# A routed expert block on one core: first biases turned on VectorE, a bias product inside the loop, last rows by a one-hot product, and a gather without empty places

## The reference, cut to what matters

```
logits = h @ router_w + router_b          # 512 x 32
top_val, top_idx = top_k(logits, 4)       # four experts for each token
gate = softmax(top_val)
for each expert e, on its tokens:
    u = h[tokens] @ w1[e] + b1[e]         # 1024 -> 2048, first bias
    g, lin = min(u[:, :1024], 7), clip(u[:, 1024:], -7, 7)
    y = ((lin + 1) * g * sigmoid(1.702 * g)) @ w2[e] + b2[e]
    out[tokens] += gate * y
x = x + g2 * out                          # g2 comes from the condition vector
```

## Time and profile before

| | us |
|---|---|
| median of 3 runs | 2125.63 (2125.32 to 2132.86) |
| profiled execution, its own time | 2124.19 |
| its span | 2122.5 |
| TensorE busy | 1951.7 (92%) |
| VectorE / ScalarE / GpSimd busy | 639.0 / 365.9 / 195.5 |
| granted clock, mean over the span | 0.965 |

### The profile page before, as it was taken

How to read it: one execution, slowest core, us unless ns; L and a number is a source line. 1 busy time by engine, 2 the same in 40 slices (tenths; PEclk the granted TensorE clock), 3 DMA queues, 4 the chain that set the end, 5 groups by cost and what they waited for, 6 DMA issues and landing times.

```text
span 2122.5 us, 37796 instructions
## 1 busy us (share of the span) xinstructions
PE 1951.7 (92%) x15926; PEld 1045.7 (49%) x15926; DVE 639.0 (30%) x1668; ACT 365.9 (17%) x823; POOL 195.5 (9%) x240
## 2 busy tenths in 40 slices
PE   5999999998999999999998888889898888989989
PEld 4576655753444444444343433434343343765854
DVE  6346757322120202122121111202020115257240
ACT  2115631432110101011000000101000011142110
POOL 1020000000002121211111111110101010000000
PEclk8979999999899999999999999999999989999999
DMA  9711222321579999999999999999999984200001
GB/s 301 225 47 60 80 80 80 159 75 64 204 258 385 384 390 374 385 380 361 383 370 377 377 372 376 371 374 369 376 369 370 339 263 130 80 1 1 1 0 40
DMA packets 155314, 510.96 MB, mean 241 GB/s; under 512 B 22098, under 2 KB 99272, under 8 KB 105992
## 3 DMA queue, kind: packets, MB, share of 16 engines
q1 hardware_dynamic: 132112, 472.94, 60.2%
q0 software_dynamic: 17088, 26.48, 5.8%
q10 hardware_dynamic: 5944, 9.09, 1.2%
HBM read 489.47 MB, written 18.48 MB: 239 GB/s over the span
## 4 chain that ended last, share of the span: by engine, by line
PE 63%; SPq 15%; DMA 14%; DVE 4%; issue 2%; ACT 1%; POOL 0%; ACTq 0%; DVEq 0%; POOLq 0%
PE bank L1417 14%; DMA ring<-in_exp_w_dram 13%; PE bank L390 10%; PE bank L1433 8%; PE bank L398 7%; SPq L888 7%; PE bank L793 5%; SPq L892 4%; PE bank L552 3%; SPq L883 3%; PE bank L574 2%; PE bank L563 2%; PE bank L764 1%; PE bank L374 1%; DVE arena L740 1%
## 5 line engine op out<-in xcount | busy, mean ns | idle before, releaser
L1417 PE MATMUL bank<-ring,arena 128*32 128x512 f32 x5696 | 643.0, 600 | 72.3 <-DMA ring<-in_exp_w_dram 69.0
L1417 PEld LDWEIGHTS bank<-ring,arena 128*32 128x32 f32 x5696 | 180.0, 111 | 511.7 <-issue 359.2
L1433 PE MATMUL bank<-ring,arena 128*32 128x256 f32 x5696 | 325.3, 386 | 24.5 <-DMA ring<-in_exp_w_dram 15.9
L1789 DVE COPY arena<-bank 128x12 f32<-128x12 f32 (+2 forms) x32 | 5.4, 170 | 911.9 <-PE bank L1381 880.1
L1433 PEld LDWEIGHTS bank<-ring,arena 128*32 128x32 f32 x5696 | 217.3, 111 | 122.8 <-DMA ring<-in_exp_w_dram 22.1
L390 PE MATMUL bank<-hT,ring 128*128 128x512 f32 x448 | 210.3, 622 | 13.2 <-DVE hT L770 7.5
L1036 POOL DMA_INDIRECT expert_sums<-arena,dst_r x89 | 137.9, 1550 | 380.3 <-ACT arena L1172 355.2
L398 PE MATMUL bank<-ring,hT 128*128 128x256 f32 (+1 forms) x768 | 156.4, 363 | 0.0
L390 PEld LDWEIGHTS bank<-hT,ring 128*128 128x128 f32 x448 | 87.7, 199 | 119.3 <-issue 115.8
L1154 ACT ACTIVATE arena<-bank 128x384 f32<-128x384 f32 (+2 forms) x64 | 26.5, 464 | 693.2 <-PE bank L1398 693.2
L398 PEld LDWEIGHTS bank<-ring,hT 128*128 128x128 f32 x768 | 135.6, 190 | 18.4 <-issue 2.4
(11 more groups left out here) (325 smaller groups left out, 1551.9 us busy)
## 6 DMA issues: line engine op xcount, KB each, us to landing
ring<-in_exp_w_dram SPq DMA_DIRECT2D x384, 1024.0 KB, 26.0
ring<-in_ada_w_dram SPq DMA_DIRECT2D x24, 1024.0 KB, 10.9
ring<-in_w_in_dram SPq DMA_DIRECT2D x23, 1024.0 KB, 9.9
ring<-in_w_out_dram SPq DMA_DIRECT2D x8, 1024.0 KB, 4.9
arena<-in_exp_b_dram SPq DMA_DIRECT2D x128, 64.0 KB
expert_sums<-arena POOLq DMA_DIRECT2D x5, 512.0 KB, 4.7
arena<-in_x_dram ACTq DMA_DIRECT2D x1, 2048.0 KB, 12.5
ring<-in_w_in_dram SPq DMA_DIRECT2D x8, 256.0 KB, 5.0
```

The source lines that it names most:

```text
L1417: mm = pe.matmul(bank[g][QUAD * c:QUAD * (c + 1), :].rearrange("p (h n) -> p h n", h=2), rowsT[:, k, QUAD * g:QUAD * (g + 1)], w[:, :, SW ...
L1433: mm = pe.matmul(bank[4 + g // 2][QUAD * c:QUAD * (c + 1), SW * (g % 2):SW * (g % 2 + 1)], actT[:, j, g, QUAD * q:QUAD * (q + 1)], w[:, c, :],
```

## The change

- First biases: the 128 bias transfers and SP's wait ahead of them go. Four transfers before the loop bring all of `exp_b1` as rows of experts; VectorE turns them once in blocks of 32x32 (`b1T`), and in each iteration reads the expert's number from `order_i` into a register, copies 16 columns and turns them, broadcast, into `b1_rows` (`biases`), ahead of `targets`.
- Second biases: the eight products of L1523 move into iterations 10 to 17, one in each, into bank 7, between the first layer and `spread`; VectorE adds each to the residual at the head of its iteration, and `turn_rows`, which also writes bank 7, waits for that. The eight products by the identity of L1527 become transposes.
- The last expert's rows are not scattered. ScalarE scales them into `y_last`, VectorE builds a one-hot matrix of tokens (`hot_last`), TensorE multiplies both in four row quarters into eight banks, VectorE adds these to the residual. ScalarE reads the sums back after the last but one expert's scatter; TensorE branches after VectorE's additions.
- Gather: the table holds token number minus 512 and VectorE adds 512, so an empty place gives 512, beyond the bound of 511, and the gather leaves it out. `xg` is zeroed once.

```diff
-            def bias_in(e, n, signal):
-                for c in range(4):
-                    sp.dma_start(b1_all[n][QUAD * c:QUAD * (c + 1), :].rearrange("p (e h n) -> p e h n", e=1, h=2),
-                                 b1_cols[c, bass.ds(e, 1), :, :].unsqueeze(0).to_broadcast([QUAD, 1, 2, SW]))\
-                      .then_inc(signal, 16)
...
-            bias_in(0, 0, b1_in[0])
+            for c in range(4):
+                sp.dma_start(b1_rows[QUAD * c:QUAD * (c + 1), :].rearrange("p (h n) -> p h n", h=2), b1_cols[c])\
+                  .then_inc(b1_in, 16)
...
-                if n >= 2:
-                    sp.wait_ge(main.u_in, n - 1)
-                bias_in(e, n % 2, b1_in[n % 2])
...
-                pool.indirect_dma_start(xg[0:rows, :], None, h2_dram, bass.IndirectOffsetOnAxis(src_i[0:rows, 0:1], 0))\
+                pool.indirect_dma_start(xg[0:rows, :], None, h2_dram, bass.IndirectOffsetOnAxis(src_i[0:rows, 0:1], 0),
+                                        bounds_check=S - 1, oob_is_err=False)\
                     .then_inc(sg.got, 16)
...
+            link(pool.memset(xg, 0.0))
...
-                if n >= 1:
+                if 1 <= n < NEXP:
                     put(main, n, PARTS_BY[n - 1], dst_r[(n - 1) % 4], QUADS[n - 1])
...
-            act.wait_ge(main.free, NEXP)
+            act.wait_ge(main.dst, NEXP)
+            act.wait_ge(main.y, NEXP)
+            for g in range(QUADS[-1]):
+                act.activation(y_last[:, g, :], bank[4 + g // 2][:, SW * (g % 2):SW * (g % 2 + 1)], ACT.Copy,
+                               scale=meta_r[(NEXP - 1) % 4][:, g, 2:3]).then_inc(y_last_ok, 1)
+            act.wait_ge(main.free, NEXP - 1)
...
+                if n in B2_AT:
+                    t = n - B2_AT[0]
+                    pe.wait_ge(main.at_ok, 2 * n)
+                    pe.matmul(bank[7][:, :], b2_keep[:, P * t:P * (t + 1)], gatesT, start=True, stop=True)\
+                      .then_inc(b2_t, 1)
...
+                    if n in B2_AT:
+                        pe.wait_ge(b2_ok, n - B2_AT[0] + 1)
                     turn_rows(main, 16 * (n + 2), QUADS[n + 1])
...
-            pe.wait_ge(main.y_ok, PARTS_BY[NEXP])
+            pe.wait_ge(main.u_in, NEXP)
+            pe.wait_ge(main.at_ok, 2 * NEXP)
+            pe.wait_ge(hot_last_ok, 1)
+            pe.wait_ge(y_last_ok, QUADS[-1])
+            for j in range(2):
+                for g in range(QUADS[-1]):
+                    for c in range(4):
+                        rows = slice(QUAD * c, QUAD * (c + 1))
+                        mm = pe.matmul(bank[2 * c + j][:, :], y_last[rows, g, P * j:P * (j + 1)], hot_last[rows, g, :],
+                                       start=(g == 0), stop=(g == QUADS[-1] - 1))
+                mm.then_inc(last_t, 1)
+            pe.wait_ge(last_ok, ND)
...
-            pe.wait_ge(gT_ok, 1)
-            for t in range(ND):
-                pe.matmul(bank[t][:, :], b2_keep[:, P * t:P * (t + 1)], gatesT, start=True, stop=False)
...
-                    mm = pe.matmul(bank[t][:, i * P:(i + 1) * P], y_rows[i][:, P * t:P * (t + 1)], ident[:, :],
-                                   start=False, stop=(i == NT - 1))
+                    mm = pe.transpose(bank[t][:, i * P:(i + 1) * P], y_rows[i][:, P * t:P * (t + 1)], ident[:, :])
...
-            dve.tensor_copy(route[:, :, :, 0], tb)
+            dve.tensor_scalar(route[:, :, :, 0], tb, -float(S), None, ALU.add)
...
-                dve.tensor_copy(src_i[0:rows, :], meta[0:rows, 0:1]).then_inc(sg.src, 1)
+                dve.tensor_scalar(src_i[0:rows, :], meta[0:rows, 0:1], float(S), None, ALU.add).then_inc(sg.src, 1)
...
+            def biases(sg, e):
+                settle(sg, dve.tensor_copy(b1_one.unsqueeze(2), b1T[:, :, bass.ds(e, 1)]))
+                settle(sg, dve.transpose(b1_rows.rearrange("p (k q) -> p k q", q=QUAD),
+                                         bc(b1_one.unsqueeze(2), [P, 16, QUAD])))
...
+            dve.wait_ge(b1_in, 64)
+            link(dve.transpose(b1T.rearrange("p k e -> p (k e)"), b1_rows))
             for n in range(NEXP):
+                if n in B2_AT:
+                    t = n - B2_AT[0]
+                    dve.wait_ge(b2_t, t + 1)
+                    dve.scalar_tensor_tensor(out=resT[:, t, :], in0=bank[7][:, :], scalar=mod[:, 40 + t:41 + t],
+                                             in1=resT[:, t, :], op0=ALU.mult, op1=ALU.add).then_inc(b2_ok, 1)
+                if n == 0:
+                    e = 0
+                else:
+                    e = dve.value_load(order_i[0:1, n:n + 1], min_val=0, max_val=NEXP - 1)
+                biases(main, e)
...
+            to_last = meta_r[(NEXP - 1) % 4]
+            for g in range(QUADS[-1]):
+                for i in range(NT):
+                    ins = dve.tensor_scalar(hot_last[:, g, P * i:P * (i + 1)], iota_c[:, :], float(P * i), to_last[:, g, 1:2],
+                                            ALU.add, ALU.is_equal)
+            ins.then_inc(hot_last_ok, 1)
+            dve.wait_ge(b2_ok, ND)
+            for j in range(2):
+                dve.wait_ge(last_t, j + 1)
+                for t in range(j, ND, 2):
+                    dve.scalar_tensor_tensor(out=resT[:, t, :], in0=bank[t][:, :], scalar=mod[:, 40 + t:41 + t],
+                                             in1=resT[:, t, :], op0=ALU.mult, op1=ALU.add).then_inc(last_ok, 1)
```

More of the change, by code:

```diff
@@ L166, in two_block_layer @@
         route = room(4608, [NT, NEXP, 4])
-        b1_all = [room(5120 + 512 * n, [512]) for n in range(2)]
+        b1T, b1_rows, b1_one = room(5120, [16, NEXP]), room(5632, [512]), room(7808, [16])
         u_in = room(OM + 1024, [4, 512])
+        y_last, hot_last = u_in[:, 0, :].rearrange("p (g n) -> p g n", g=2), u_in[:, 2:4, :]
         posmT = room(OM + 1024, [S], NEXP)
@@ L273, in two_block_layer @@
         w1_used, w2_used = sem("w1_used"), sem("w2_used")
-        b1_in = [sem("b1_in0"), sem("b1_in1")]
+        b1_in = sem("b1_in")
         places_in, repl_ok, pos_ok, perm_ok, turned_ok, order_ok = (
@@ L281, in two_block_layer @@
         y_used = sem("y_used")
+        b2_t, b2_ok = sem("b2_t"), sem("b2_ok")
+        hot_last_ok, y_last_ok, last_t, last_ok = (sem(n) for n in ("hot_last_ok", "y_last_ok", "last_t", "last_ok"))
         f_t, f_ok, f_out = sem("f_t"), sem("f_ok"), sem("f_out")
@@ L825, in dve_out @@
                 ins.then_inc(res_ok, 1)
+        B2_AT = range(10, 10 + ND)
+        assert QUADS[-1] == 2
         OUT_PARTS = ((0, 4), (4, 6), (6, 8))
@@ L1793, in targets, with swiglu @@
                 dve.tensor_tensor(dst[:, 0:quads], dst_f[:, 0:quads], slot_base[:, 0:quads], ALU.add).then_inc(sg.dst, 1)
-            def swiglu(sg, n, bias, quads):
+            def biases(sg, e):
+                settle(sg, dve.tensor_copy(b1_one.unsqueeze(2), b1T[:, :, bass.ds(e, 1)]))
+                settle(sg, dve.transpose(b1_rows.rearrange("p (k q) -> p k q", q=QUAD),
+                                         bc(b1_one.unsqueeze(2), [P, 16, QUAD])))
+            def swiglu(sg, n, quads):
                 for g in range(quads):
-                    ins = dve.tensor_tensor(u_in[:, g, :], bank[g][:, :], bias, ALU.add)
+                    ins = dve.tensor_tensor(u_in[:, g, :], bank[g][:, :], b1_rows, ALU.add)
                 ins.then_inc(sg.u_in, 1)
@@ L1890, in _ @@
                     at = dve.value_load(pos_i[0:1, 0:1], min_val=0, max_val=NEXP - 1)
+                    of = dve.value_load(exp_i[0:1, 0:1], min_val=0, max_val=NEXP - 1)
+                    biases(over, of)
                     dve.tensor_copy(route_o[:, :, :], route[:, :, bass.ds(at, 1), :].rearrange("p i e c -> p i (e c)"))
@@ L1898, in _ @@
                     targets(over, o + 1, meta_r[0], dst_r[0], 4)
-                    dve.wait_ge(over_in, o * (16 * (SLOTS + 4)) + 16 * (SLOTS + 4))
+                    dve.wait_ge(over_in, o * (16 * SLOTS) + 16 * SLOTS)
                     dve.wait_ge(over.u, o + 1)
-                    swiglu(over, o + 1, b1_all[0], 4)
+                    swiglu(over, o + 1, 4)
             dve.wait_ge(y_used, NT)
```

16 lines of the change are left out of this document (8 added, 8 removed).

## The result

The changed kernel takes 2053.62 us, the median of four runs (2049.77 to 2055.15), against 2125.48 for the kernel before on the same chip (2125.16 to 2132.86). The ratio is 0.9651, with a 95% interval of 0.9626 to 0.9676: 3.5% faster, a gain of 72 us where the sum above has 32.4. The profiled execution took 2054.17 us, its span is 2052.4.

The account below looks back on a forecast made before the run. TensorE was taken to bind up to about 960 us, the DMA engines after. 24.5 + 5 - 4 - 2 + 8.9 = 32.4 us off 2124.19 gave 2091.8, forecast as 2093 us, range 2072 to 2114.

Parts of the forecast that it names:

- What bounds the kernel: Expert loop: TensorE binds to about 960 us, DMA engines after; at most 85 us can be won by relieving DMA.
- Part 1: Expert loop: 7680 bias packets of 1 KB leave the DMA engines, at 51 ns each 24.5 us won.
- rival A: Whole kernel: relief passes whole, with even engines, nothing lost early and fast transposes; 45 us won, 2079; chance 0.15.
- Part 2: Gather in the expert loop: 800 empty rows of 4 KB skipped, 0 to 10 us won, 5 taken.
- rival D: Gather: leaving places out puts the rest on fewer engines and weights wait; slower, 2156; chance 0.05 with an unseen cause 0.06.
- Part 3: Loop up to about 960 us: TensorE binds, so part of the saved DMA time is lost; 4 us written off.
- Part 4: Iterations 10 to 17: bias product delays the second layer 2.2 us each, 18 over eight, mostly covered; 2 us charged.
- a cover of 19: Iterations 10 to 17: TensorE's idle time, 27 us, shrinking to 19 after the DMA relief, hides the bias product's stall.
- Part 5: Tail after the last expert product: one-hot product and transposes take 20.5 us against 29.4; 8.9 us won.
- 36 as the sign for the forecast: Expert loop after 1001 us: twelve weight slots in about 36 us instead of 37.2 would show the forecast right.
- B's picture: Iterations 10 to 17: TensorE takes over, waits for VectorE replace ring waits; 2111, at the upper end 2121; chance 0.12.
- C: Expert loop: small packets cost nothing, slipping in between weights, so only the tail is won; 2117; chance 0.07.

Follow-up runs that it names:

- every_fourth: The kernel before with its four bias transfers an expert each written to every fourth of 128 partitions instead of 32 neighbours; 2084.04 us, ratio 0.9794.
- tail_and_b2_only: The kernel before with only the second biases' product in iterations 10 to 17 and the new tail, biases and gather as before; 2117.8 us, ratio 0.9943.
- after_b2_late: The changed kernel with the second biases' product in iterations 22 to 29 and VectorE's biases step ahead of its wait for it; 2050.9 us, ratio 0.9627.
- own_rows_32: The kernel before with each partition of the four bias transfers reading another expert's bias, still into 32 neighbouring partitions; 2126.95 us, ratio 1.0001.
- bias_only: The kernel before with only the first biases held in SBUF and turned on VectorE; 2066.73 us, ratio 0.9705.
- after_hoist: The changed kernel with only VectorE's biases step moved ahead of its wait for the second biases' product; 2050.76 us, ratio 0.9640.
- gather_all_128: after_hoist with every gather issued over all 128 partitions, added places left out by the bounds check; 2036.31 us, ratio 0.9568.

## Why the prediction fell short

**What bounds the kernel: right.** The loop was bound by the DMA engines from 960 us on, the 85 us of ring waits were the ceiling, and 67 of them went. But the sentence that four issues fewer save "only what their packets cost the engines" is where the error enters: it has no room for a cost that a packet puts on others. (Its 120 issues are right for the loop; 124 went in all, four of them ahead of it.)

**Part 1, the bias transfers: the step that failed.** The term was 24.5 us, from 51 ns a packet taken in a stretch in which nothing but 1 KB packets flew. Measured: 62.7 in all, of which the packets' own part is 20 (by bytes I had 21), and 43 are weights slowed beside them. Neither the forecast nor rival A had this in it, since both multiply a packet's own time. I took the price of the packets from a stretch without weights, and read the share of 1.03 as useful work; but it is the same at 373 and at 393 GB/s, so it also counts what a packet loses to others. The trace of before could have told. These are the 15 us slices of GB/s from 1001 to 1601 us, first of before, then of every_fourth:

```profile
GB/s 352 420 336 390 372 370 398 350 400 349 379 383 359 386 341 398 397 355 390 343 386 385 360 393 345 386 373 369 382 359 398 362 368 381 357 375 359 379 389 353
```
```profile
GB/s 388 419 389 386 390 387 393 397 421 383 393 389 385 392 397 421 379 399 386 388 389 399 421 386 386 382 388 382 399 418 372 398 386 385 381 397 415 378 402 386
```

Before dips to 336 to 353 every few slices; every_fourth, with the same bias packets, never goes under 372. Finer stretches of before tell what the dips are. I cut 1001 to 1601 us into pieces of 3 us and leave out those with traffic of queue 0 (gathers and scatters, a share of 1% or more). The 48 pieces without packets of 1 KB (fewer than five) carry 418 GB/s in the mean, the 53 with them 367. From 1136 to 1139 us, for one, it is 426, and from 1139 to 1142, where 102 of these packets fly, 338. In every_fourth the same means are 417 and 420 (40 and 59 pieces). 53 pieces are 9.9 us for each of 16 experts; at a rate 12% lower that is 1.2 us an expert, 38 over 31 of them, an estimate that leaves out the pieces with gathers and comes near the 43.

On VectorE's side the estimates held: the transpose took 0.71 us (0.65 taken), and the register load left no gap that the trace shows, L1883 ending at 1004.23 and the copy L1822 starting at 1004.22, where I had put 1.0.

**Part 2, the gather: right in size,** 4.7 us (interval 2.3 to 7.2) for the 5 taken. The 800 rows are gone as bytes, but each leaves a packet under 512 B, which the sum did not have. That leaving places out might load few engines (rival D) did not come true. That the gather's destinations cost another 15 us was not in it, and the change doesn't touch that.

**Part 3, TensorE early: right in kind.** 700 to 960 us is at 257.7 of 260 us, no better than before. The 4 us written off for it were not measured by themselves.

**Part 4, the bias product: the cover was wrong, the 2 us are not refuted.** I charged 2 us against a cover of 19. With the relief of 63 instead of 24.5 the cover was gone: TensorE is busy 255.8 us of 260 in 960 to 1220. In tail_and_b2_only, with the weights still the bound, the stall shows no loss (12.1 us won, 9.9 of them in the tail). The stall was shorter than computed, 1.4 us over the usual gap instead of 2.2, but the iterations had a second price that I did not write down: a granted clock of 0.50 for some 3 us, and second layers 1.7 us longer, in all eight (three of eleven are so without the product, in after_b2_late). That is at most 3.1 us an iteration, 25 in all, against a cover that was no longer there. The medians have no more than 5 of them as lost gain (79.5 against 74.2), and taking the product out of these iterations (after_b2_late) gave no more than 5 either. That the slots that filled meanwhile were used later is the likely reason.

**Part 5, the tail: right.** 9.6 us won for 8.9, with the one-hot passes at 0.116 us, VectorE's sums at 5.36 and the transposes 1.2 us faster than taken (5.83 us at a mean clock of 0.63, at 0.50 for the first half). The next layer's weights did not come late.

**Rivals and signs.** Twelve slots take 600 / 217 x 12 = 33.2 us; I had named 36 as the sign for the forecast, and 37.2 for no effect. TensorE's ring waits are 18 us, not 50. By my own list that is beyond the forecast towards B's picture, waits for VectorE in their place (10.7 us), but at a gain no case had. A, at 2079 the nearest, is 25 us above the measured time; C, packets at no cost, has the costly term at nothing. The range was too narrow because its good end, A, was built from the same term as the forecast: I priced the term from a stretch of small packets alone and by its bytes at the mean rate, and neither holds what the weights lose beside it.

## What to carry to other kernels

Where transfers share saturated engines, price a small transfer by what the big ones lose, not by its own packets: two sets of short stretches of one trace, with and without it, and the GB/s at an unchanged share show it (418 and 367 here). Give side transfers destinations that spread over all 128 partitions, even by every fourth partition or with a list of places that are left out. And when a change relieves one bound by more than a few per cent, recompute every edit that was hidden under it. All of this is one kernel's evidence.

## What the runs showed of the hardware

- A transfer into 32 neighbouring partitions slows the weight stream beside it: 256 KB an expert cost 20 us over the kernel by their bytes and 43 more by where they land (373 against 393 GB/s; in pieces of 3 us 367 with them and 418 without). Gathers over 64 and 96 partitions cost 15 us against gathers over 128 with the same rows; whether by where they land or by how they are dealt out isn't shown.
- A place of a gather that the bounds check leaves out moves no row but still costs a packet under 512 B: 800 and 1248 such places, 800 and 1248 more of these packets.
- A share of 1.03 over 16 engines goes with 369 (own_rows_32), 373 (before), 394 (bias_only) and 396 GB/s (after_hoist) alike; it doesn't tell how well an engine works, and at 1.02 it went with 403 (gather_all_128).
- Reading one 2 KB row pair for 32 or 128 partitions costs no more than reading distinct rows (ratios 1.0001 and 0.9801 beside 0.9799).
- Behind the bias product (32 contracted rows, 1.1 us) the second layer ran at a lower granted clock in most iterations (8 of 8, 6 of 8 and 7 of 8 in three kernels): 8.80 us for 128 passes instead of 7.11, 12.25 for 192 instead of 10.57. In after_b2_late's iterations without it, 3 of 11 did. In the one looked at closely the clock was at 0.50 (1.2 GHz) for some 3 us, after 9 us of work at 1.00 and a wait of 0.53 us.
- Products of 32 contracted rows in four row quarters run at 0.116 us for 512 columns, against 0.44 on the whole array.
